# Attention heads of a one-core transformer kernel: TensorE transposes replaced by VectorE block transposes and ScalarE copies

## The reference

```python
ya = moba_attention(qa, ka, va).reshape(B, S, W_A) * jax.nn.silu(za)          # 8 heads of 128, causal
yb = dilated_mixture(qb, kb, vb).reshape(B, S, W_B_OUT) * jax.nn.silu(zb)     # 4 heads, 3 groups of keys each
ym = memory_attention(qm, mk, mv).reshape(B, S, W_M) * jax.nn.silu(zm)        # 4 heads of 256, no mask
merged = g_a * (ya @ w_proj_a) + g_b * (yb @ w_proj_b) + g_m * (ym @ w_proj_m)
```

## Time and profile before

| | |
|---|---|
| median of 3 timed runs | 2194.4 us (2193.51 to 2196.37) |
| span of the profiled execution, first to last instruction | 2190.4 us |
| lowest timed run less the span | 3.1 us |
| TensorE busy | 2177.8 us, 99% |
| VectorE busy | 1323.6 us, 60% |
| ScalarE busy | 1029.2 us, 47% |
| TensorE clock granted, mean | 1.000 of full speed |

### The profile page before, as it was taken

One profiled execution on the slowest core, in us unless ns is written; L12 is line 12 of the kernel. 1 busy time (PEld: TensorE's weight loads), 2 busy tenths in 40 slices (PEclk: granted clock), 3 DMA queues, 4 the chain that ended last, 5 costly groups with the idle time before them and its releaser, 6 DMA issues.

```text
span 2190.4 us, 25672 instructions
## 1 busy us (share of the span) xinstructions
PE 2177.8 (99%) x9870; PEld 1806.4 (82%) x9870; DVE 1323.6 (60%) x1608; ACT 1029.2 (47%) x1241; POOL 154.3 (7%) x260
## 2 busy tenths in 40 slices
PE   9999999999999999999999999999999999999998
PEld 7788888888888888888888888888888888888887
DVE  5865656676455646545676878665555555554444
ACT  6544444444444444444545666454444444444443
POOL 0010101011000000000111100120001000100000
PEclk9999999999999999999999999999999999999999
DMA  8676656577754657668878756687777777776654
GB/s 302 206 234 176 203 172 208 184 231 238 206 163 149 209 180 229 198 206 285 260 240 284 230 183 200 196 267 230 219 211 225 216 211 212 226 229 203 193 193 154
DMA packets 229731, 468.89 MB, mean 214 GB/s; under 512 B 16632, under 2 KB 16896, under 8 KB 228736
## 3 DMA queue, kind: packets, MB, share of 16 engines
q1 hardware_dynamic: 212128, 409.00, 60.4%
q0 software_dynamic: 17056, 57.69, 8.7%
q10 hardware_dynamic: 448, 0.86, 0.1%
HBM read 439.69 MB, written 27.79 MB: 213 GB/s over the span
## 4 chain that ended last, share of the span: by engine, by line
PE 97%; DVE 2%; DMA 0%; ACT 0%; issue 0%; ACTq 0%; DVEq 0%
PE ps L1549 31%; PE ps L1551 31%; PE ps L1550 31%; PE ps L1448 1%; PE ps L1470 1%; DVE w_lo L916 1%; DVE ps L1266 1%; PE ps L1417 1%; PE ps L1459 0%; DMA raw<-in_w_in 0%; PE ps L1582 0%; PE ps L1583 0%; PE ps L1581 0%; PE ps L1487 0%; PE ps L1519 0%
## 5 line engine op out<-in xcount | busy, mean ns | idle before, releaser
L916 DVE TENSOR_TENSOR w_lo<-raw,w_hi 128x1024 fp32r<-128x1024 f32 (+1 forms) x776 | 931.8, 1211 | 730.4 <-ACT w_hi L605 729.2
L605 ACT ACTIVATE w_hi<-raw 128x1024 fp32r<-128x1024 f32 (+1 forms) x776 | 811.2, 1050 | 910.9 <-PE ps L1551 836.5
L1549 PE MATMUL ps<-w_hi,xT_hi 128*128 128x512 f32 x1088 | 429.8, 395 | 0.0
L1551 PE MATMUL ps<-w_hi,xT_lo 128*128 128x512 f32 x1088 | 424.1, 390 | 0.0
L1550 PE MATMUL ps<-w_lo,xT_hi 128*128 128x512 f32 x1088 | 423.6, 389 | 0.0
L1549 PE MATMUL ps<-w_hi,u2T_hi 128*128 128x512 f32 x704 | 273.9, 389 | 0.0
L1550 PE MATMUL ps<-w_lo,u2T_hi 128*128 128x512 f32 x704 | 273.9, 389 | 0.0
L1551 PE MATMUL ps<-w_hi,u2T_lo 128*128 128x512 f32 x704 | 273.9, 389 | 0.0
L1551 PEld LDWEIGHTS ps<-w_hi,xT_lo 128*128 128x128 f32 x1088 | 204.2, 188 | 43.2
L1550 PEld LDWEIGHTS ps<-w_lo,xT_hi 128*128 128x128 f32 x1088 | 204.5, 188 | 41.0
L1549 PEld LDWEIGHTS ps<-w_hi,xT_hi 128*128 128x128 f32 x1088 | 204.4, 188 | 41.1 <-issue 0.6
(11 more groups left out here) (260 smaller groups left out, 2288.4 us busy)
## 6 DMA issues: line engine op xcount, KB each, us to landing
raw<-in_w_in SPq DMA_DIRECT2D x368, 512.0 KB, 4.4
raw<-in_w_ffn_gate SPq DMA_DIRECT2D x88, 512.0 KB, 4.4
raw<-in_w_ffn_up SPq DMA_DIRECT2D x88, 512.0 KB, 4.6
raw<-in_w_ffn_down SPq DMA_DIRECT2D x88, 512.0 KB, 4.7
raw<-in_w_out SPq DMA_DIRECT2D x64, 512.0 KB, 5.8
bounce<-tmp POOLq DMA_DIRECT2D x45, 512.0 KB, 3.4
stage<-bounce POOLq DMA_DIRECT2D x140, 128.0 KB, 5.2
raw<-in_w_mem_kv SPq DMA_DIRECT2D x32, 512.0 KB, 5.3
```

The costliest lines, as they stand in the source:

```text
L605: nc.scalar.activation(w_hi[:, s, 0:per], raw[:, s, 0:per], ACT.Copy).then_inc(hi_ready, 1)
L916: nc.vector.tensor_tensor(w_lo[:, s, 0:per], raw[:, s, 0:per], w_hi[:, s, 0:per].bitcast(F32), ALU.subtract)\
L1549: nc.tensor.matmul(bank(2 * par + t), x_hi, w_hi[:, s, k], start=first, stop=False)
L1551: ins = nc.tensor.matmul(bank(2 * par + t), x_lo, w_hi[:, s, k], start=False, stop=last)
```

## The change

Each head now works like this. VectorE scales the exponentials by the row's inverse sum before they are turned (`unit_turn`, now VectorE's), transposes them in blocks of 32x32 into `probsT`, and ScalarE puts the blocks in their places with 16 copies of 32 partitions each, from `probsT` back to `scores` (`unit_probs`), in three or four pieces with a chunk's `w_hi` between them. TensorE multiplies with the values stationary, so the result comes out already transposed, and neither the probabilities nor the result pass through TensorE transposes. VectorE then multiplies by the gate (`unit_y`), which must now be transposed too: the five gate tiles get the kind `siluT` and travel through the bounce. The scores of one query block are made with one product over 256 keys instead of two over 128.

The positions change: scores stay after chunk 0; VectorE turns at 6 (5 for dilated heads), ScalarE copies at 7, 8, 9 (6 to 9 for dilated heads), TensorE multiplies with the values after 7, and `unit_y`, `unit_hi`, `unit_lo` come in the next tile. Dilated heads start at chunk 4 of tiles 21 to 24; their gate tile moves ahead of the three value tiles. Later counts of bounces rise by 5.

```diff
-            ten += [dict(w=w_in, col=VB + NW * g, x="x", post=("take", vb[:, g])) for g in range(3)]
-            ten += [dict(w=w_in, col=ZB, x="x", post=("silu", zb[:, :, :]))]
+            ten += [dict(w=w_in, col=ZB, x="x", post=("siluT", zbT, 0))]
+            ten += [dict(w=w_in, col=VB + NW * g, x="x", post=("take", vb[:, g])) for g in range(3)]
...
+        def units_in_tiles():
+            out_ = [(4 + n, 0, mem_unit(n)) for n in range(4)]
+            out_ += [(8 + n, 0, moba_unit(n)) for n in range(8)]
+            return out_ + [(21 + n, 4, dil_unit(n)) for n in range(4)]
...
-            def unit_copy(unit):
-                act.wait_ge(u_pT, w("u", 1))
-                for t in range(NT):
-                    a, n = sb_at(unit, t)
-                    ins = nc.scalar.activation(probsT[:, a:a + n], ps[:, unit["p_at"][t]:unit["p_at"][t] + n], ACT.Copy)
+            def unit_probs(unit, first, last):
+                n = n_blocks(unit)
+                turned = probsT[:, 0:n * P].rearrange("p (m b a) -> p m b a", m=4, a=32)
...
+                if first == 0:
+                    act.wait_ge(u_turned, unit["n"] + 1)
+                for k in range(first, last):
+                    m, g = k // 4, k % 4
+                    src = turned[32 * g:32 * (g + 1), m]
...
+                        dst = to[32 * m:32 * (m + 1), :, 32 * g:32 * (g + 1)]
+                    ins = nc.scalar.activation(dst, src, ACT.Copy)
+                if last == 16:
+                    ins.then_inc(u_probs, 1)
...
+            for i, o, unit in units_in_tiles():
+                place(tiles, "act_hooks", i, o + 4, lambda unit=unit: unit_exp(unit))
+                if unit["whole"]:
+                    cuts, at_ = (0, 6, 11, 16), o + 7
+                else:
+                    cuts, at_ = (0, 4, 8, 12, 16), o + 6
+                for k, (a, b) in enumerate(zip(cuts, cuts[1:])):
+                    place(tiles, "act_hooks", i, at_ + k, lambda unit=unit, a=a, b=b: unit_probs(unit, a, b))
+                place(tiles, "act_hooks", i, o + (13 if unit["whole"] else 12), lambda unit=unit: unit_hi(unit))
...
+            def unit_turn(unit):
+                dve.wait_ge(u_exp, unit["n"] + 1)
+                link(nc.vector.reciprocal(rinv, rowsum))
+                link(nc.vector.tensor_tensor(rinv, rinv, R["x"]["r"], ALU.mult))
+                for t in range(NT):
+                    a, n = sb_at(unit, t)
+                    ins = nc.vector.tensor_scalar(scores[:, a:a + n], scores[:, a:a + n], rinv[:, t:t + 1], None, ALU.mult)
+                link(ins)
+                n = n_blocks(unit)
+                if unit["whole"]:
+                    ins = nc.vector.transpose(probsT[:, 0:n * P], scores[:, 0:n * P].rearrange("p (b m a) -> p m b a", m=4, a=32))
...
+            for i, o, unit in units_in_tiles():
+                whole = bool(unit["whole"])
+                place(tiles, "dve_hooks", i, o + 4, lambda unit=unit: unit_mask(unit))
+                place(tiles, "dve_hooks", i, o + (6 if whole else 5), lambda unit=unit: unit_turn(unit))
+                place(tiles, "dve_hooks", i, o + (12 if whole else 11), lambda unit=unit: unit_y(unit))
+                place(tiles, "dve_hooks", i, o + (13 if whole else 12), lambda unit=unit: unit_lo(unit))
...
-            def unit_turn(unit):
-                pe.wait_ge(u_exp, w("u", 1))
...
-                        ins = nc.tensor.transpose(ps[:, o:o + P], scores[:, a + c:a + c + P], ident)
...
             def unit_values(unit):
-                pe.wait_ge(u_pTc, w("u", 1))
...
+                pe.wait_ge(u_probs, unit["n"] + 1)
+                if unit["n"]:
+                    pe.wait_ge(u_y, unit["n"])
...
+                for d in range(unit["width"] // P):
+                    for n, ((_, _, v), kt, p0, a, b) in enumerate(unit["values"]):
+                        ins = nc.tensor.matmul(bank(7, d * S + a, d * S + b), v(kt)[:, d * P:(d + 1) * P], scores[:, p0:p0 + b - a],
+                                               start=n == 0, stop=n == len(unit["values"]) - 1)
-            def unit_y(unit):
-                pe.wait_ge(u_y, w("u", 1))
-                transposes(lambda t, c: y_tok[:, t, c * P:(c + 1) * P], unit["y_at"], unit["width"] // P).then_inc(u_yT, 1)
...
+            for i, o, unit in units_in_tiles():
+                place(tiles, "pe_hooks", i, o, lambda unit=unit: unit_scores(unit))
+                place(tiles, "pe_hooks", i, o + 7, lambda unit=unit: unit_values(unit))
```

More of the change, by code:

```diff
@@ L100, in count_post @@
         self.step(f"a{prev['par']}")
-        if prev["post"][0] in ("silu", "ffg"):
+        if prev["post"][0] in ("silu", "siluT", "ffg"):
             self.step("z")
 def bounced(kind):
-    return (kind[0] in ("turn", "ffu") or kind[0] == "rope" or kind[0] == "mix" and kind[2] == "last"
+    return (kind[0] in ("turn", "siluT", "ffu") or kind[0] == "rope" or kind[0] == "mix" and kind[2] == "last"
             or kind[0] == "res" and kind[3] != "out")
@@ L297, in dil_unit, with n_blocks, place @@
                      lambda kt, g=g: vb[:, g, kt, j * HD:(j + 1) * HD]) for g in range(3)]
[L298 to L300 removed]
+            return dict(n=3 * QUAD + j, turned=18, z_turned=19, scale=HD ** -0.5,
+                        blocks=[[(s, 0) for s in srcs], [(s, kt) for s in srcs for kt in range(2)]],
+                        width=HD, mask=("dil0", "dil1"), s_at=(4 * NW, 5 * NW),
+                        values=[v for g, s in enumerate(srcs) for v in ((s, 0, 3 * P * g, 0, S), (s, 1, 3 * P * g + S, P, S))],
+                        zT=zbT[:, j:j + 1], kc=8 + j, whole=None, copied=None)
+        def n_blocks(unit):
+            return sum(len(b) for b in unit["blocks"])
+        def place(tiles, key, i, h, f):
+            while h >= len(chunks(tiles[i])):
+                i, h = i + 1, h - len(chunks(tiles[i]))
+            tiles[i].setdefault(key, {}).setdefault(h, []).append(f)
+        def units_in_tiles():
+            out_ = [(4 + n, 0, mem_unit(n)) for n in range(4)]
+            out_ += [(8 + n, 0, moba_unit(n)) for n in range(8)]
+            return out_ + [(21 + n, 4, dil_unit(n)) for n in range(4)]
         def sb_at(unit, t):
@@ L396, in tiles_out @@
             three, four = res_tiles(w_out, "m", x1, 1, what="u")
-            return cut_pair([one, two, far(three, 20), far(four, 21)], 19)
+            return cut_pair([one, two, far(three, 25), far(four, 26)], 24)
         def merge_last(n):
@@ L408, in late_in @@
                 return 2
-            return 9 if len(chunks(tile)) > 9 else 3 if late and (late[0][1] or late[0][0][0] in ("res", "turn") or late[0][0][0] == "rope" and late[0][0][-1] == "late") else 1
+            return 9 if len(chunks(tile)) > 9 else 3 if late and (late[0][1] or late[0][0][0] in ("res", "turn", "siluT") or late[0][0][0] == "rope" and late[0][0][-1] == "late") else 1
         def ffn_last(n):
@@ L434, in tiles_out2 @@
             three, four = res_tiles(w_out2, "y2", h2, 1, what="u2")
-            one, two, three, four = far(one, None), far(two, 31), far(three, 32), far(four, 33)
+            one, two, three, four = far(one, None), far(two, 36), far(three, 37), far(four, 38)
             return [cut(one, 0, 0, 6, True), cut(two, 1, 0, 6, False), cut(one, 0, 6, 7, False), cut(two, 1, 6, 7, False),
@@ L769, in run @@
                         post(prev, h + 1)
[L770 to L773, removed]
                     if "lru" in tile and h == 5:
@@ L1207, in run @@
                         f()
-                if unit and unit_chunk(tile, h) == 7:
-                    unit_norm(unit)
-                    unit_lo(unit)
                 if "lru" in tile:
@@ L1553, in run @@
                     w.step("g")
-                    if unit and unit_chunk(tile, h) in at_:
-                        (unit_scores, unit_turn, unit_values, unit_y)[at_.index(unit_chunk(tile, h))](unit)
                     if "ret" in tile and h == 0:
```

192 lines of the change are left out of this document (88 added, 104 removed).

## The result

The changed kernel takes 2224.95 us (median of 4 runs, 2222.86 to 2227.27) where the kernel before took 2193.95 (4 runs) in the same comparison: ratio 1.0145, 95% interval 1.0133 to 1.0157. It is slower by 1.45%, 31 us; the prediction was 2191 us, with a range of 2183 to 2200. The profiled execution has a span of 2225.5 us.

A forecast was written before the change was run, and what follows sets the result against it. TensorE, busy 99% of the span, was taken to bound the kernel. From the 2190.4 us span, 15.8 of TensorE gain came off and 12.4 of stalls were added: 2187.0, plus 4.0 from span to median, 2191 us; range 2183 to 2200.

The forecast's parts named there:

- Gain on TensorE, 15.8 us: TensorE over all heads: 13.7 us from removed transposes, 1.0 from old waits gone, 1.1 from regrouped score products.
- The rival of dear transposes: TensorE: each removed transpose costs its 272 ns duration, 31.6 us in place of 13.7, giving 2173 us; chance 0.02.
- The chain up to the turned probabilities, 15.5 us in tile 9: VectorE's masking, rotation, scaling and transposing in tile 9: probabilities turned 15.5 us after the scores start.
- where TensorE wants the values, 19.73: Tile 9 on TensorE: chunk 7 ends, and the probabilities are wanted, 19.73 us after the scores start.
- A copy of 96 elements 0.19 us, of 128 0.22, of 288 0.35: ScalarE's small copies of probabilities: price each, from 0.84 ns a column and 0.20 us fixed, 0.1 of it overlapping.
- the prediction's own sign: ScalarE's copies: prediction wrong if they are spaced by 0.25 us or more, waits name `w_lo`, or waits are absent.
- The rival of dear copies: ScalarE: a 128-element copy costs up to 0.31 us, adding 15.8 us over 11 heads, giving 2207 us; chance 0.15.
- No term for the clock: TensorE's stalls before the values were summed at 12.4 us, with nothing added for a lower granted clock.
- The gate tiles' extra transfers at nothing: Five gate tiles: added VectorE transpositions, a bounce and a ScalarE copy costed at nothing; without cover, engine parts 11.7 us.
- `w_lo` late: Rival: VectorE's turning delays chunk 7's `w_lo`; large products wait 0.1 to 0.5 us in seven tiles, 2192 to 2194.5; chance 0.06.
- the eleven named: Heads where TensorE was to wait on copies: tiles 5, 6, 9, 10, 13, 14, 15 and all four dilated heads.
- "about 1 us" of cover: Tiles 8, 11, 12, without a rotation ahead: copies ready by 18.7 us, so no stall and about 1 us spare.

## Why the prediction was wrong, step by step

- *Gain on TensorE, 15.8 us.* Right: 14.8 to 15.8 by the kernel with one copy and the later take. That a transpose costs 0.11 us of stream and not its 272 ns held. The rival of dear transposes is out.
- *The chain up to the turned probabilities, 15.5 us in tile 9, and where TensorE wants the values, 19.73.* Both right to 0.1 us, and with `w_lo` of chunk 6 at 12.81 for 12.84 the prices of VectorE on the way too.
- *A copy of 96 elements 0.19 us, of 128 0.22, of 288 0.35, "of which 0.1 overlaps in a row": the first step that failed.* Start to start is 0.293 for 96, and busy equals duration, 0.308 and 0.442, for the others. The durations were right: 0.20 and 0.84 ns a column make 0.28, 0.31 and 0.44 us, and 0.281, 0.308 and 0.442 were measured. Only the overlap was wrong. It came from rows whose instructions all begin at partition 0; the copies begin in another quadrant each time, and with that the 0.1 is gone. In tile 9 this is 16 x 0.10 for the copies and 0.2 for the pieces of `w_hi` behind them: 1.0 + 1.8 = 2.8 us in place of 1.0; measured are a wait of 2.51 us and 347.54 − 344.9 = 2.6 between the two blocks. Over all heads the waits became 29.9 us instead of 12.4. With the source kept in one quadrant, where three copies of four overlap, they were 14.8, near the predicted 12.4. By the prediction's own sign ("copies are spaced by 0.25 or more") this step failed.
- *Ends of the range for that price.* The rival of dear copies had it as high as 0.31 for 128 elements, which is about what came (0.308 busy, nothing overlapped), with 2207 us as its result and "45 ns makes it slower". Its 15.8 us are most of the 17.5 by which the waits grew; the other 15 us, the clock, it lacked as well. I gave it 0.15 since the copies are "nearest in kind" to an ordinary copy, and looked only at operation and memory, not at where they start.
- *No term for the clock: the second step that failed.* The sum took a wait at its own length. Behind nine of the twelve waits TensorE ran at 1.2 GHz, 15 us in all. By where the sum went wrong: 17.5 us of longer waits and 15 of clock are 32.5, and 2191 + 32.5 = 2223.5 for 2224.95 measured. That it closes so well is partly luck. It leaves out 2.4 us more of waits for `w_lo`, and the 4.0 us between span and median were not time around the program: 2227.27 of the profiled execution less its span of 2225.5 is 1.8, and with the same 1.8 the execution profiled before took 2192.2, against a median of 2194.4.
- *The gate tiles' extra transfers at nothing; `w_lo` late.* In the changed kernel so: none of its 4.1 us of waits for `w_lo` lies beside a head. Without the long waits for the copies it is no longer so: `w_lo` is late by 4.2 us beside heads with the values later, and by 8.3 with one copy, where a take held by its transfer had a part in it. The rival was real but hidden behind a larger wait.
- *Which tiles wait.* Right for 4, 7, 11, 12 and the eleven named; tile 8, expected free with "about 1 us" of cover, waited 0.6 us. The 1.8 us of extra copying is more than that cover; why tiles 11 and 12, which were given the same cover, didn't wait was not looked into.

On the overlap, the Trainium skill (ScalarE: Activation LUTs, What ACT_TABLE_LOAD costs) says that back-to-back ACTIVATEs overlap by about 93 ns, measured on tiles of 128 partitions. The trace agrees where the quadrants stay (96-element copies 265 to 283 ns long start 0.17 to 0.19 us apart) and contradicts it where one changes (281 ns long and busy for 281). The Trainium skill (VectorE: DVE Perf Modes, Two Vector instructions with no wait between them) describes such a hold, by the start quadrant of input and output, for VectorE alone; the changed kernel and the two runs with other quadrants show the same pattern on ScalarE.

Left open: exactly when a wait brings the clock down. Of waits of equal length some are followed by a stretch at 1.2 GHz and some aren't. Tile 9's, 2.51 us, was. In the run with the copies in another order, whose waits are the same within 0.03 us, it was the other way round: the clock fell at tile 13's and not at tile 9's. Tile 13's in the execution of the changed kernel, on TensorE and in the clock of the windows behind it:

```profile
449.13 0.92 PE L1503 MATMUL ps<-scores,va 128*128 128x256 f32 x4 [2.49 <-ACT scores L681]
```

```profile
450.00:451.00 1.00, 1.00 (x6) 0.82 (x5) 0.81 (x1) 1.00 (x2) 0.00 (x0) 1.00 0.94 195
451.00:452.00 1.00, 1.00 (x6) 0.80 (x6) 1.00 (x2) 1.00 (x2) 0.00 (x0) 1.00 0.86 315
```

Nor was the take's wait traced beyond the bounce: that the weights' transfers delay it was not tried.

## What to carry to other kernels

An instruction's overlap with its neighbour is a property of the pair: price a small copy from a row whose neighbour also starts in another quadrant, and if there is none, take duration for spacing, which for 16 copies of 32 partitions is 1.8 us a head more. On the engine that sets the time, a wait costs its length and possibly the clock behind it: nine of the eleven waits of 2.0 to 3.3 us took about 1.7 more here, so first look for a place a chunk later for what waits (one line, 37 us here). And when one wait is removed, ask again what the engine meets next: with the values moved, the take one chunk later was worth another 3.3 us (the take alone, on the changed kernel, was not run). Both moves together, 2184.07 us, give the fastest kernel here that makes all its copies, 0.4% under the one before.

## What the runs showed of the hardware

- ScalarE: two instructions in a row overlapped by about 0.09 us only when source and destination began in the same quadrants as those of the one before. With the source or the destination changed the next one began some 12 ns after the end of the last (0.281 us long, 0.293 apart); the same held for a `w_hi` of 128 partitions behind a copy that had written another quadrant.
- Granted clock: at waits of TensorE beside the heads of 1.9 us or more it fell to 1.2 GHz in 20 of 26 cases over the ten profiled executions: at all seven of 3.26 us and longer, at 13 of the 19 between 1.89 and 2.94, and at none of 1.8 us or less. It fell between 0.7 us before the wait's end and 1.5 us after it, and stayed low for 3.4 us, once for 6.8. With the wait filled by useless products it stayed at 2.4 GHz, and 14.8 us came back.
